# A two-block transformer forward pass: the first keys and values formed chunk by chunk while the modulation weights arrive

## The chip, the cores and the metric

The kernel runs on one core of a Trainium2 chip. TensorE multiplies matrices, ScalarE (ACT in the profile) applies functions, VectorE (DVE) does elementwise work, GpSimd (POOL) copies, and SyncE (SP) issues most of the DMAs. The metric is the device time of one execution in microseconds (us).

## What is computed

Two model blocks follow each other on 256 tokens of width 1024. The first has two layers, each with attention, a long convolution, gates and a feed-forward part, and works on `x` and on 256 context tokens. The second ends in a mixture of 32 experts. The change concerns the very start of layer 0, cut from the reference here:

```python
mod = (silu_c @ w_mod[layer] + b_mod[layer])[:, None, :]
mod_c = silu_cc @ w_mod[layer] + b_mod[layer]
shift1, scale1, gate1, shift2, scale2, gate2 = jnp.split(mod, N_MOD, axis=-1)
h_ctx = modulate(rms_norm(ctx, norm_mix[layer]), c_shift1, c_scale1)   # h*(1+scale)+shift
qc, kc, vc, hyc, gc = jnp.split(h_ctx @ w_in[layer], PROJ_SPLITS, axis=-1)
h = modulate(rms_norm(x, norm_mix[layer]), shift1, scale1)
q, k, v, hy, g = jnp.split(h @ w_in[layer], PROJ_SPLITS, axis=-1)
```

## The kernel before

Activations lie with features on the partitions: `X` is 8 chunks of 128 features by 512 tokens (`x` and the context side by side), 2 MB. Every engine has its own program, written by hand in order, and engines meet by semaphores; nothing is reordered.

**The modulation.** `shift1` and `scale1` need 16 columns of 128 of `w_mod`. They come as 16 units of 512 KB (`first`), into `area`, `HH` and `KX`. Four units make a group: `pe_mod_group` multiplies the two conditions by them (8 matmuls, L629), ScalarE copies the result (`ac_mod_group`, L653), and `pe_mod_turn` turns it into columns (4 matmuls, L645). Groups 0 and 1 hold the eight shift columns, groups 2 and 3 the eight scale columns, so no chunk of `X` can be modulated before group 3 is turned. Then `ve_mod_groups` adds the bias (L662) and forms the scale (L669).

**The norm.** ScalarE squares the eight chunks (L575), VectorE adds seven of them (L551), TensorE sums over features (L535, L542), ScalarE takes the root (L587), VectorE the reciprocal (L598), TensorE spreads it (L558), and VectorE multiplies each chunk of `X` into `H` (L882).

**A chunk's last steps.** ScalarE scales and shifts it in two halves (L863). GpSimd (L875), or for chunks 2 and 5 ScalarE (L868), rounds it to the high part `HH`. VectorE forms the low part `HL` (L890). A projection is three matmuls for each product: high by high, high by low, low by high.

**The weights** of the projections come as 512 KB units through a ring of six places. ScalarE makes the high part of each unit in one of three places (`his`, L453), VectorE the low part (L461). Units 0 and 1 are the keys' weights, 2 and 3 the values', 4 on the queries'. A place comes free when the product that read it is done.

**The projections.** `pe_idle` first runs 12 matmuls on ones, whose result nobody reads (L570). `pe_pair` forms both key heads over the eight chunks (6 matmuls of 512 columns for each chunk, L497), `pe_head_sums` sums the squares of key head 0 (L521), `pe_values_projected` forms the values (12 matmuls of 256 columns for each chunk, L948), and a second sum follows. Then come the eight query heads, 24 matmuls each (L482).

**The loads.** SyncE issues in this order: four units of `w_mod`, `X` whole, eight units of `w_mod`, units 0 and 1 of `w_in`, four of `w_mod`, unit 2, the constants of the transforms (1347 KB), units 3 to 5, then two tables into `area` for the filter.

## Time and profile before

| | |
|---|---|
| Median of 3 runs | 2072.62 us (2068.78 to 2075.53) |
| The profiled execution's own time | 2071.54 us |
| Its span | 2069.7 us |
| TensorE busy | 1880.4 us, 91% |
| VectorE busy | 1155.6 us, 56% |
| ScalarE busy | 903.6 us, 44% |
| DMA moved | 428.01 MB, 207 GB/s over the span |
| First key matmul starts | 40.06 us |

The span runs from the first to the last instruction, and 1.8 us of the execution's time lie around it. A busy TensorE is not one at full rate: its clock has two levels, shown as granted clock 1.00 (2.4 GHz) and 0.50 (1.2 GHz). Times below count from the start of the span. An fp32 matmul shows as two instructions in the rows, so "x8" there is four matmuls.

### The profile page before, as it was taken

The numbers are of one execution on the slowest core, as the hardware profiler recorded it, in microseconds if no ns is written. First come the engines' busy times: TensorE is split into PE (matmuls) and PEld (weight loads), VectorE is DVE, ScalarE is ACT, GpSimd is POOL, SyncE is SP. The second block draws the span as 40 slices with busy tenths as digits, with TensorE's granted clock in tenths as the row PEclk, the third lists the DMA queues.
The fourth block names the chain that finished last, engine by engine and source line by source line (L and its number), as shares of the span: only waits on it lengthen the run. The fifth ranks groups of instructions, "written<-read, shape, count | busy, mean of one in ns | idle before, by whom it ended". The sixth has DMA issues, their size and how long they took to land.

```text
span 2069.7 us, 33760 instructions
## 1 busy us (share of the span) xinstructions
PE 1880.4 (91%) x14150; PEld 1547.8 (75%) x14150; DVE 1155.6 (56%) x1898; ACT 903.6 (44%) x1532; POOL 17.0 (1%) x31
## 2 busy tenths in 40 slices
PE   7999989999999999999999999999999777767666
PEld 4877668888778888798699999997898544445444
DVE  3555767775887788567666667689764111110012
ACT  4333446665766677455455556644844000000001
POOL 0000000000000000000000000000000000000000
PEclk8999999999999999999999999999999998998888
DMA  8222024553555555224056555543248999999996
GB/s 315 92 72 82 1 72 157 181 184 106 175 175 181 195 192 174 101 93 153 1 184 204 180 187 194 175 159 107 92 143 340 419 420 421 419 419 420 420 421 249
DMA packets 91121, 428.01 MB, mean 207 GB/s; under 512 B 11089, under 2 KB 12754, under 8 KB 66002
## 3 DMA queue, kind: packets, MB, share of 16 engines
q1 hardware_dynamic: 78866, 382.51, 49.5%
q10 hardware_dynamic: 12096, 43.26, 6.2%
q8 instruction: 114, 1.87, 0.4%
q14 instruction: 45, 0.37, 0.1%
HBM read 424.68 MB, written 1.05 MB: 206 GB/s over the span
## 4 chain that ended last, share of the span: by engine, by line
PE 65%; DMA 19%; DVE 8%; ACT 5%; issue 2%; SPq 1%; ACTq 0%; DVEq 0%
PE bank L482 42%; DMA area<-in_w 8%; PE bank L1629 8%; DMA his<-in_w 4%; DMA ring<-in_w 4%; DMA PPT<-in_w 3%; PE bank L497 2%; PE bank L2518 2%; PE bank L2474 1%; DVE st L1280 1%; PE bank L1208 1%; ACT PPT L1225 1%; PE bank L948 1%; DVE ring_r L461 1%; PE bank L2125 1%
## 5 line engine op out<-in xcount | busy, mean ns | idle before, releaser
L461 DVE TENSOR_TENSOR ring_r<-ring,his_r 128x1024 fp32r<-128x1024 f32 x314 | 383.3, 1223 | 220.9 <-ACT his_r L453 219.6
L482 PE MATMUL bank<-HH_r,his_r 128*128 128x256 f32 (+1 forms) x1504 | 497.1, 331 | 2.5 <-DVE ring_r L461 2.5
L482 PE MATMUL bank<-HH_r,ring_r 128*128 128x256 f32 (+1 forms) x1504 | 489.3, 325 | 0.0
L482 PE MATMUL bank<-H_r,his_r 128*128 128x256 f32 (+1 forms) x1440 | 470.3, 327 | 0.0
L453 ACT ACTIVATE his_r<-ring 128x1024 fp32r<-128x1024 f32 x314 | 330.8, 1056 | 292.8 <-PE bank L482 262.6
L482 PEld LDWEIGHTS bank<-HH_r,his_r 128*128 128x128 f32 x1504 | 284.4, 189 | 35.0 <-issue 9.6
L482 PEld LDWEIGHTS bank<-HH_r,ring_r 128*128 128x128 f32 x1504 | 284.2, 189 | 24.8
L482 PEld LDWEIGHTS bank<-H_r,his_r 128*128 128x128 f32 x1440 | 271.4, 188 | 25.2 <-issue 1.0
L2490 DVE TENSOR_TENSOR tmp<-tmp,bank 128x128 f32<-128x128 f32 x64 | 18.4, 288 | 385.3 <-ACT tmp L2483 255.3
L482 PE MATMUL bank<-area_r,his_r 128*128 128x256 f32 (+1 forms) x480 | 148.3, 321 | 0.0
L2474 PE MATMUL bank<-area,KF 128*32 128x128 f32 x1888 | 88.1, 308 | 38.2 <-DMA area<-in_w 33.2
L1629 PE MATMUL bank<-VT_r,his_r 128*128 128x512 f32 (+1 forms) x352 | 117.2, 333 | 0.3 <-DVE YF_r L1360 0.3
L1629 PE MATMUL bank<-YF_r,his_r 128*128 128x512 f32 (+1 forms) x352 | 117.0, 333 | 0.0
L1629 PE MATMUL bank<-VT_r,ring_r 128*128 128x512 f32 (+1 forms) x352 | 117.0, 333 | 0.0
L2474 PEld LDWEIGHTS bank<-area,KF 128*32 128x32 f32 x1888 | 71.4, 124 | 51.9 <-DMA area<-in_w 41.9
L482 PEld LDWEIGHTS bank<-area_r,his_r 128*128 128x128 f32 x480 | 90.4, 191 | 6.9
L2529 ACT ACTIVATE H<-bank 128x512 f32<-128x512 f32 x16 | 9.6, 598 | 193.5 <-PE bank L2518 193.5
L731 ACT ACTIVATE rst<-rst 128x1024 f32<-128x1024 f32 x80 | 83.6, 1046 | 1.7 <-DVE rst L723 1.6
L2518 PE MATMUL bank<-area,tmp 128*32 128x512 f32 x256 | 59.3, 682 | 19.1 <-DMA area<-in_w 18.7
L1629 PEld LDWEIGHTS bank<-VT_r,his_r 128*128 128x128 f32 x352 | 66.1, 188 | 7.3 <-DVE YF_r L1360 0.5
L1629 PEld LDWEIGHTS bank<-YF_r,his_r 128*128 128x128 f32 x352 | 66.1, 188 | 6.9
L1629 PEld LDWEIGHTS bank<-VT_r,ring_r 128*128 128x128 f32 x352 | 66.1, 188 | 6.9
(415 smaller groups left out, 3309.2 us busy)
## 6 DMA issues: line engine op xcount, KB each, us to landing
area<-in_w SPq DMA_DIRECT2D x91, 1024.0 KB, 27.5
ring<-in_w_in SPq DMA_DIRECT2D x102, 512.0 KB, 3.5
ring<-in_w_gate_up SPq DMA_DIRECT2D x88, 512.0 KB, 3.5
ring<-in_w SPq DMA_DIRECT2D x36, 1024.0 KB, 27.3
HH<-in_w SPq DMA_DIRECT2D x26, 1024.0 KB, 26.7
ring<-in_w_down SPq DMA_DIRECT2D x44, 512.0 KB, 3.5
KX<-in_w_mod_rows ACTq DMA_DIRECT2D x28, 512.0 KB, 3.4
VX<-in_w_mod_rows ACTq DMA_DIRECT2D x28, 512.0 KB, 3.5
```

The lines of the kernel that those rows point to most:

```text
L453: ac.eng.activation(hi_slot(n), stream.slot(u), ACT.Copy).then_inc(*ac_hi.up(n))
L461: ve.eng.tensor_tensor(lo_slot(u), stream.slot(u), hi_slot(n).bitcast(F32), ALU.subtract).then_inc(*ve_lo.up(n))
L482: ins = pe.eng.matmul(out, a, b, start=k == 0 and m == 0, stop=end)
L497: ins = pe.eng.matmul(out, a, b, start=k + m == 0, stop=k == 7 and m == 2)
L731: ac.eng.activation(prod, prod, ACT.Copy, accum_out=MODS[l][:, j, s:s + 1]).then_inc(*ac_mod.up("sum", n, s))
L948: ins = pe.eng.matmul(vb[tb // 2][:, o:o + 256], x[:, k, sl], w, start=k == 0 and n == 0 and o == 0, stop=k == 7 and n == 2 and o > 0)
L1208: ins = pe.eng.matmul(out[:, 0:256], vs(kc), c.pts[g % 2][:, kc * 256:(kc + 1) * 256], start=kc == 0, stop=kc == c.nk - 1)
L1225: ac.eng.activation(p[:, m * w:(m + 1) * w], src[:, m * w:(m + 1) * w], ACT.Exp, bias=st[:, so + m:so + m + 1], scale=c.rq(h, i + m) if c. ...
L1280: ve.eng.reduce_max(st[:, so:so + c.n], src.rearrange("p (a b) -> p a b", a=c.n), AX.X, negate=True).then_inc(*ve_soft.up("max", c.site, h ...
L1629: ins = pe.eng.matmul(banks.ap("ff", l, 4 * half + n)[:, 0:t], w, x, start=k == 0 and i == 0, stop=k == 21 and i == 2)
L2474: ins = pe.eng.matmul(out[32 * n:32 * n + 32, 0:P], HG[g % 2][:, k, 32 * j:32 * j + 32], w, start=k == 0, stop=k == 7, tile_position=(0, 3 ...
L2518: ins = pe.eng.matmul(out[32 * j:32 * j + 32, :], AT[j][:, 32 * k:32 * k + 32], w, start=k == 0, stop=k == 3, tile_position=(0, 32 * j))
```

## The change

Six things are changed, all before or in the first projections of layer 0; layer 1 and the rest keep their order.

- **Groups.** The columns of `w_mod` are permuted (`FIRST_MOD`), so that group g holds shift and scale of chunks 2g and 2g+1. `ve_mod_first` forms these after each turn: three small instructions a group, twelve in place of three.
- **Loads.** `X` comes first, in two halves. Units 0 and 1 of `w_in` follow the first group, unit 2 the second, unit 3 the third. The transforms' constants come behind unit 5, and the filter's tables wait for group 3, since `w_mod` lies where they go.
- **Places.** `w_mod` no longer uses `HH`, which is written early now; it uses `area`, `VX` and `KX`. The high parts of units 3, 4 and 5 get places of their own in `VT` and `KF`, which stand idle until the convolution filter.
- **Order.** `pe_start`, `ac_start` and `ve_start` replace the written-out beginning. Keys and values go side by side, chunk by chunk, between the modulation's groups.
- **Dummy work.** `pe_idle` is not called.
- **Sums of the keys.** Both follow query head 0 (i = 2) in place of standing around the values, and the root, the reciprocal and the spreading move one head later.

```diff
+HIGH_ELSEWHERE = range(NHI, 2 * NHI)
+FIRST_MOD = [j for g in range(4) for j in (2 * g, 2 * g + 1, 8 + 2 * g, 9 + 2 * g)]
...
-        first = Stream([("w_mod", 0, u) for u in range(16)], [area[:, i * UF:(i + 1) * UF] for i in range(11)] +
-                       [hh_flat[:, i * UF:(i + 1) * UF] for i in range(4)] + [KX_flat[:, :]], [sem(f"s_m{i}") for i in range(16)], UB)
+        first = Stream([("w_mod", 0, u) for u in range(16)], [area[:, i * UF:(i + 1) * UF] for i in range(14)] + [VX_flat[:, :], KX_flat[:, :]], [sem(f"s_m{i}") for i in range(16)], UB)
...
         def hi_slot(n):
-            at = n % NHI * UW + stream.leads[cut_units[n]]
+            lead = stream.leads[cut_units[n]]
+            if n in HIGH_ELSEWHERE:
+                tile, at = ((VTR, 0), (KFR, 0), (KFR, UF))[n - NHI]
+                return tile.rearrange("p a t -> p (a t)")[:, at + lead:at + lead + UF]
+            at = n % NHI * UW + lead
             return his[:, at:at + UF]
+
+        def hi_before(n):
+            return n - NHI if n >= 3 * NHI else n - 2 * NHI
...
-            if g > 0:
-                pe_mod_turn(pe, g - 1)
-            if g == 3:
-                pe_mod_turn(pe, g)
-                banks.give("mods")
...
-        def ve_mod_groups(ve):
-            ve.wait_ge(*pe_mod.at("turn", 3))
-            ve_mod_bias(ve, 0, 0, 16, banks.ap("mods")[:, 0:32].rearrange("p (j s) -> p j s", s=2))
-            ve_mod_scale(ve, 0, 0)
+        def ve_mod_first(ve, g):
+            chunks = slice(2 * g, 2 * g + 2)
+            src = banks.ap("mods")[:, 0:32].rearrange("p (w k s) -> p w k s", w=2, s=2)
+            dst = MODS[0][:, 0:16, :].rearrange("p (w k) s -> p w k s", w=2)
+            bias = vv(("b_mod", 0), 0, 16).rearrange("p (w k) -> p w k", w=2)
+            ve.wait_ge(*pe_mod.at("turn", g))
+            for w in range(2):
+                ve.eng.tensor_tensor(dst[:, w, chunks, :], src[:, w, chunks, :], bias[:, w, chunks].unsqueeze(2).to_broadcast([P, 2, 2]),
+                                     ALU.add).then_inc(*ve_mod.up(*(("first", g) if w else ("shift", g))))
+            ve.wait_ge(*ve_mod.last())
+            ve.eng.scalar_tensor_tensor(A12S[0][:, 0, chunks, :], dst[:, 1, chunks, :], 1.0,
+                                        vv(("norm_mix", 0), 2 * g, 2).unsqueeze(2).to_broadcast([P, 2, 2]), ALU.add,
+                                        ALU.mult).then_inc(*ve_mod.up("first_scale", g))
...
+        def pe_start(pe):
+            pe_mod_group(pe, 0)
+            pe_open(pe, "mix0")
+            pe_added("mix0")
+            pe.wait_ge(*gp_start.at("ones"))
+            pe_sum_seven(pe, "mix0", 512)
+            pe_sum_last(pe, "mix0", 512)
+            pe_mod_turn(pe, 0)
+            pe_spread(pe, "mix0", 512)
+            pe_mod_group(pe, 1)
+            keys = [(("head", 0, i), head_bank(pe, 0, i), 8 * pos[8 + i]) for i in range(2)]
+
+            def pe_keys_chunk(k):
+                pe_pair_chunk(pe, keys, "w_in", 0, k, lambda k: (HH[:, k, 0:512], HL[:, k, 0:512]),
+                              lambda k: pe.wait_ge(*ve_norm.at("low", "mix0", k)))
+
+            pe_keys_chunk(0)
+            pe_keys_chunk(1)
+            pe_mod_turn(pe, 1)
+            pe_values_open(pe, 0)
+            pe_values_chunk(pe, 0, 0)
+            pe_values_chunk(pe, 0, 1)
+            pe_mod_group(pe, 2)
+            for k in range(2, 8):
+                pe_keys_chunk(k)
+                pe_values_chunk(pe, 0, k)
+                if k == 2:
+                    pe_mod_turn(pe, 2)
+                    pe_mod_group(pe, 3)
+                if k == 3:
+                    pe_mod_turn(pe, 3)
+
+        def ac_start(ac):
             for k in range(8):
...
+                ac.wait_ge(*landed[f"x{k // 4}"])
+                ac_square(ac, "mix0", k, X[:, k, :], 512)
+            ac_sqrt_table(ac, 5, 8)
+            ac_mod_group(ac, 0)
+            ac_split(ac, where["w_in", 0, 0])
+            ac_sqrt(ac, "mix0", 8, 512, 1024)
+            ac_split(ac, where["w_in", 0, 1])
+            ac_first_chunk(ac, 0)
+            ac_first_chunk(ac, 1)
+            ac_mod_group(ac, 1)
+            ac_split(ac, where["w_in", 0, 2])
+            ac_first_chunk(ac, 2)
+            ac_first_chunk(ac, 3)
+            ac_split(ac, where["w_in", 0, 3])
+            ac_mod_group(ac, 2)
+            ac_first_chunk(ac, 4)
+            ac_mod_group(ac, 3)
+            for k in (5, 6, 7):
+                ac_first_chunk(ac, k)
+            ac_split(ac, where["w_in", 0, 5])
+
+        def ac_first_chunk(ac, k):
+            ac.wait_ge(*ve_mod.at("first_scale", k // 2))
+            ac_norm_chunk(ac, "mix0", 0, 512, k)
+
+        def ve_start(ve):
+            for k in range(1, 7):
+                ve_add_square(ve, "mix0", k, 512)
+            ve_reciprocal(ve, "mix0", 512)
+            ve_split(ve, where["w_in", 0, 0])
+            ve_mod_first(ve, 0)
+            ve_split(ve, where["w_in", 0, 1])
+            r = spread_out(ve, "mix0", 512)
+            for k in range(4):
+                ve_scaled(ve, "mix0", k, 512, r)
+            ve_norm_low(ve, "mix0", 512, 0)
+            ve_norm_low(ve, "mix0", 512, 1)
+            ve_scaled(ve, "mix0", 4, 512, r)
+            ve_scaled(ve, "mix0", 5, 512, r)
+            ve_split(ve, where["w_in", 0, 2])
+            ve_mod_first(ve, 1)
+            ve_scaled(ve, "mix0", 6, 512, r)
+            ve_scaled(ve, "mix0", 7, 512, r)
+            ve_norm_low(ve, "mix0", 512, 2)
+            ve_norm_low(ve, "mix0", 512, 3)
+            ve_split(ve, where["w_in", 0, 3])
+            ve_mod_first(ve, 2)
+            ve_norm_low(ve, "mix0", 512, 4)
+            ve_mod_first(ve, 3)
+            for k in (5, 6, 7):
+                ve_norm_low(ve, "mix0", 512, k)
+            ve_split(ve, where["w_in", 0, 5])
...
         def pe_heads(pe, l):
-            pe_pair(pe, [(("head", l, i), head_bank(pe, l, i), 8 * pos[8 + i]) for i in range(2)], "w_in", l,
-                    lambda k: (HH[:, k, 0:512], HL[:, k, 0:512]), lambda k: pe.wait_ge(*ve_norm.at("low", f"mix{l}", k)))
-            pe_head_sums(pe, l, 0)
-            pe_values_projected(pe, l)
-            pe_head_sums(pe, l, 1)
+            if l:
+                pe_pair(pe, [(("head", l, i), head_bank(pe, l, i), 8 * pos[8 + i]) for i in range(2)], "w_in", l,
+                        lambda k: (HH[:, k, 0:512], HL[:, k, 0:512]), lambda k: pe.wait_ge(*ve_norm.at("low", f"mix{l}", k)))
+                pe_head_sums(pe, l, 0)
+                pe_values_projected(pe, l)
+                pe_head_sums(pe, l, 1)
             for i in range(2, 10):
                 pe_head(pe, l, i)
-                if i < 4:
-                    pe_spread(pe, head_site(l, i - 2), 512)
+                if l == 0 and i == 2:
+                    pe_head_sums(pe, l, 0)
+                    pe_head_sums(pe, l, 1)
+                if 3 - l <= i < 5 - l:
+                    pe_spread(pe, head_site(l, i - 3 + l), 512)
...
-            ac_sqrt(ac, head_site(l, 0), 1, 512, P)
+            if l:
+                ac_sqrt(ac, head_site(l, 0), 1, 512, P)
...
             for i in range(2):
                 ve_split(ve, two_on(unit("w_in", l, 8 * pos[heads(l)[i][0]])))
-            ve_reciprocal(ve, head_site(l, 0), 512)
+            if l:
+                ve_reciprocal(ve, head_site(l, 0), 512)
             ve_rope_step(ve, l, 0)
             for b in (10, 11):
                 ve_split(ve, two_on(unit("w_in", l, 8 * pos[b])))
-            ve_reciprocal(ve, head_site(l, 1), 512)
+            if l:
+                ve_reciprocal(ve, head_site(l, 1), 512)
             ve_rope_step(ve, l, 1)
+            if l == 0:
+                ve_split(ve, two_on(unit("w_in", l, 8 * pos[0])))
+                for i in range(2):
+                    ve_reciprocal(ve, head_site(l, i), 512)
             for i in range(2, 10):
                 ve_split(ve, two_on(unit("w_in", l, 8 * pos[heads(l)[i][0]])))
-                if i < 4:
-                    ve_key(ve, l, i - 2)
+                if 3 - l <= i < 5 - l:
+                    ve_key(ve, l, i - 3 + l)
...
-            pe_mod_group(pe, 0)
-            pe_mod_group(pe, 1)
-            pe_open(pe, "mix0")
-            pe_added("mix0")
-            pe.wait_ge(*gp_start.at("ones"))
-            pe_sum_seven(pe, "mix0", 512)
-            pe_sum_last(pe, "mix0", 512)
-            pe_spread(pe, "mix0", 512)
-            pe_mod_group(pe, 2)
-            pe_mod_group(pe, 3)
-            pe_idle(pe, "mix0", 12)
+            pe_start(pe)
...
-            ac_mod_group(ac, 0)
-            ac.wait_ge(*landed["x"])
-            for k in range(8):
-                ac_square(ac, "mix0", k, X[:, k, :], 512)
-            ac_mod_group(ac, 1)
-            ac_sqrt_table(ac, 5, 8)
-            ac_sqrt(ac, "mix0", 8, 512, 1024)
-            ac_mod_group(ac, 2)
-            ac_split(ac, where["w_in", 0, 1])
-            ac_mod_group(ac, 3)
-            ac_norm_mod(ac, "mix0", 0, 512)
+            ac_start(ac)
...
-            for k in range(1, 7):
-                ve_add_square(ve, "mix0", k, 512)
-            r = ve_rstd(ve, "mix0", 512)
-            for k in range(8):
-                ve_scaled(ve, "mix0", k, 512, r)
-            ve_split(ve, where["w_in", 0, 1])
-            ve_mod_groups(ve)
-            ve_norm_mod(ve, "mix0", 0, 512)
+            ve_start(ve)
...
+            for half in range(2):
+                sp.eng.dma_start(X[:, 4 * half:4 * half + 4, :], T["x"][:, 4 * half:4 * half + 4, :]).then_inc(*landed[f"x{half}"])
             for i, (name, l, u) in enumerate(first.units):
                 if i == 4:
-                    sp.eng.dma_start(X[:, :, :], T["x"]).then_inc(*landed["x"])
-                if i == 12:
                     weights(0)
                     weights(1)
+                if i in (8, 12):
+                    weights(i // 4)
                 sp.eng.dma_start(first.slot(i), T[name][l, u]).then_inc(first.arrived(i)[0], 16)
-            weights(2)
-            sp.eng.dma_start(con[:, NCON0:NCON], T["con"][:, NCON0:NCON]).then_inc(*landed["dft"])
-            for i in range(3, len(stream.units)):
+            for i in range(4, len(stream.units)):
                 if i == NS:
+                    sp.eng.dma_start(con[:, NCON0:NCON], T["con"][:, NCON0:NCON]).then_inc(*landed["dft"])
+                    sp.wait_ge(*pe_mod.at("group", 3))
                     sp.eng.dma_start(FIN, T["fil"]).then_inc(*landed["fil0"])
                     sp.eng.dma_start(FW, T["fw"][0]).then_inc(*landed["fw0"])
...
-    arrays["w_mod"] = fours(I["w_mod"][0:1, :, 0:2048])
+    arrays["w_mod"] = fours(I["w_mod"][0:1].reshape(1, 1024, 48, P)[:, :, FIRST_MOD].reshape(1, 1024, 2048))
```

`pe_pair_chunk`, `pe_values_chunk`, `ac_norm_chunk` and `ve_norm_low` are the bodies of the old loops, for one chunk.

TensorE at the start, before, from the first turn to the first key matmul (`bank0` collects the turned columns, `HH_r` and `H_r` are high and low part of the chunks, `his_r` and `ring_r` of the weights):

```order
L645 MATMUL bank0<-con,PPT 128x2 x4
L535 MATMUL bank3<-ones,tmp2 128x1 x4
L542 MATMUL bank3<-ones,tmp1 128x1 x4
L558 MATMUL bank3<-con,st 128x128 x4
L629 MATMUL bank4<-area,sc2 32x512 x6
L629 MATMUL bank4<-HH,sc2 32x512 x2
L645 MATMUL bank0<-con,PPT 128x2 x4
L629 MATMUL bank5<-HH,sc2 32x512 x6
L629 MATMUL bank5<-KX,sc2 32x512 x2
L645 MATMUL bank0<-con,PPT 128x2 x8
L570 MATMUL bank6<-ones 128x128 x12
L497 MATMUL bank7<-HH_r_50,his_r_62 128x512
```

The same engine after, up to the fourth group:

```order
L651 MATMUL bank0<-con,PPT 128x2 x4
L569 MATMUL bank2<-con,st 128x128 x4
L640 MATMUL bank3<-area,sc2 32x512 x8
L508 MATMUL bank4<-HH_r_50,his_r_62 128x512
...
L651 MATMUL bank0<-con,PPT 128x2 x4
L977 MATMUL bank6<-his_r_62,HH_r_50 128x256
...
L640 MATMUL bank1<-area,sc2 32x512 x8
L508 MATMUL bank4<-HH_r_50,his_r_62 128x512
...
L651 MATMUL bank0<-con,PPT 128x2 x4
L640 MATMUL bank2<-area,sc2 32x512 x4
```

The first keys stand behind group 1 (`bank3`), the first values behind turn 1, two further keys and values between groups 2 and 3; before, all stood behind turn 3 and the dummy matmuls.

VectorE at the same place, before, from the reciprocal of the norm:

```order
L598 RECIPROCAL st<-st 128x4
L882 TENSOR_TENSOR H<-X,bank3 128x512 x8
L461 TENSOR_TENSOR ring_r_61<-ring,his_r_62 128x1024 x2
L662 TENSOR_TENSOR MOD0<-bank0,vec 128x32
L669 SCALAR_TENSOR_TENSOR A120<-MOD0,vec 128x8 x2
L890 TENSOR_TENSOR H_r_49<-H,HH_r_50 128x512 x8
L1023 TENSOR_SCALAR qg<-vec 128x1
```

And after, from the same reciprocal:

```order
L609 RECIPROCAL st<-st 128x4
L469 TENSOR_TENSOR ring_r_61<-ring,his_r_62 128x1024
L670 TENSOR_TENSOR MOD0<-bank0,vec 128x4 x2
L673 SCALAR_TENSOR_TENSOR A120<-MOD0,vec 128x4
L469 TENSOR_TENSOR ring_r_61<-ring,his_r_62 128x1024
L902 TENSOR_TENSOR H<-X,bank2 128x512 x4
L912 TENSOR_TENSOR H_r_49<-H,HH_r_50 128x512 x2
L902 TENSOR_TENSOR H<-X,bank2 128x512 x2
L469 TENSOR_TENSOR ring_r_61<-ring,his_r_62 128x1024
L670 TENSOR_TENSOR MOD0<-bank0,vec 128x4 x2
L673 SCALAR_TENSOR_TENSOR A120<-MOD0,vec 128x4
```

The first low parts (`H_r_49`) now stand behind two weight splits, the first group's three small instructions and four scaled chunks; before they stood behind all eight.

## Rows read from the trace of the kernel before

**Rows 1.** The page: DMA busy tenths in 40 slices, then the last chain by engine.
```profile
DMA  8222024553555555224056555543248999999996
...
PE 65%; DMA 19%; DVE 8%; ACT 5%; issue 2%; SPq 1%; ACTq 0%; DVEq 0%
```

**Rows 2.** TensorE weight loads, window 5 to 37 us: start, us, what, [idle, releaser].
```profile
9.00 0.14 PEld L629 LDWEIGHTS bank<-area,sc 128*32 128x32 f32 x4 [1.05 <-DMA area<-in_w_mod]
15.19 0.19 PEld L629 LDWEIGHTS bank<-area,sc 128*32 128x32 f32 x4 [6.05 <-DMA area<-in_w_mod]
...
19.03 0.14 PEld L629 LDWEIGHTS bank<-area,sc 128*32 128x32 f32 x4 [1.10 <-DMA area<-in_w_mod]
...
32.96 0.14 PEld L629 LDWEIGHTS bank<-KX,sc 128*32 128x32 f32 x4 [1.12 <-DMA KX<-in_w_mod]
```

**Rows 3.** ScalarE, window 13 to 37 us, same columns.
```profile
13.88 1.15 ACT L575 ACTIVATE tmp<-X 128x512 f32<-128x512 f32 x2 [3.19 <-DMA X<-in_x]
...
19.57 0.63 ACT L575 ACTIVATE tmp<-X 128x512 f32<-128x512 f32 x1 [0.16 <-DVE tmp L551]
...
20.75 1.28 ACT L580 ACT_TABLE_LOAD   x1
...
29.93 1.99 ACT L453 ACTIVATE his_r<-ring 128x1024 fp32r<-128x1024 f32 x2
```

**Rows 4.** TensorE, window 19 to 41 us, same columns.
```profile
20.93 1.03 PE L535 MATMUL bank<-ones,tmp 128*128 128x1 f32 x8
21.82 1.33 PE L542 MATMUL bank<-ones,tmp 128*128 128x1 f32 x8
23.72 2.08 PE L558 MATMUL bank<-con,st 128*128 128x128 f32 x8 [0.57 <-DVE st L598]
25.73 2.78 PE L629 MATMUL bank<-area,sc 128*32 128x512 f32 x10
...
29.30 1.05 PE L645 MATMUL bank<-con,PPT 128*128 128x2 f32 x8
30.28 1.06 PE L629 MATMUL bank<-HH,sc 128*32 128x512 f32 x8
```

**Rows 5.** VectorE, window 25 to 41 us, same columns.
```profile
25.84 4.87 DVE L882 TENSOR_TENSOR H<-X,bank 128x512 f32<-128x512 f32 x8 [2.17 <-PE bank L558]
31.08 2.36 DVE L461 TENSOR_TENSOR ring_r<-ring,his_r 128x1024 fp32r<-128x1024 f32 x2 [0.38 <-ACT his_r L453]
35.93 0.19 DVE L662 TENSOR_TENSOR MOD<-bank,vec 128x32 f32<-128x32 f32 x1 [2.49 <-PE bank L645]
36.16 0.24 DVE L669 SCALAR_TENSOR_TENSOR A<-MOD,vec 128x8 f32<-128x8 f32 x2
38.23 0.69 DVE L890 TENSOR_TENSOR H_r<-H,HH_r 128x512 fp32r<-128x512 f32 x1 [1.83 <-POOL HH_r L875]
```

**Rows 6.** Last chain, window 32 to 80 us: start, us, what.
```profile
35.89 4.41 PE bank L570 x24
40.30 10.24 PE bank L497 x45
...
52.91 11.41 PE bank L948 x96
64.33 0.78 PE bank L521 x8
65.11 5.58 PE bank L482 x24
```

**Rows 7.** Three windows: length, busy by engine, granted clock, DMA share, GB/s.
```profile
22.70:29.10 6.40, 5.83 (x27) 2.75 (x26) 3.44 (x7) 0.26 (x1) 0.00 (x0) 0.50 1.03 410
36.50:39.70 3.20, 3.20 (x18) 3.20 (x18) 0.96 (x2) 3.17 (x7) 1.44 (x2) 0.54 1.04 416
40.00:50.00 10.00, 10.00 (x47) 8.30 (x46) 5.47 (x9) 6.66 (x13) 2.91 (x4) 1.00 0.24 73
```

**Rows 8.** SyncE queue, window 1555 to 1600 us: start, us, what it issues.
```profile
1562.44 0.43 SPq L2911 DMA_DIRECT2D con<-in_w  x1
```

112 lines of the change are left out of this document (64 added, 48 removed).

## The prediction

> **What bounds the kernel now.** The page comes first. The chain that ended last is TensorE for 65% and DMA for 19%, and the row of DMA shares shows where the DMA part lies: the last nine slices are full, the middle is at a fifth to a half, and the first slice is full too [rows 1]. So there are three stretches. A filled queue bounds the start, TensorE the long middle, the experts' weights the end. The change is in the first.
>
> The start is read next, by what TensorE's weight loads wait for. The units of `w_mod` let them go at 9.0 us for the fourth, 15.2 for the fifth, 19.0 for the eighth and 33.0 for the sixteenth [rows 2]. ScalarE finds `X` landed at 13.9 us and ends the eight squares at 20.2 [rows 3]. TensorE has little to do meanwhile: sums, spreading, groups, turns [rows 4]. VectorE has scaled all of `X` by 30.7 us and then stands until the turn lets it form the scales at 35.9 [rows 5]. The last chain puts it together: dummy matmuls of 4.4 us, keys from 40.3, values, the sums of the keys, query head 0 from 65.11 to 70.69 [rows 6]. At 70.69 both key heads, their sums, the values and query head 0 are done. That mark is the one to compare: after the change the same work is done when query head 0 and the two sums behind it are.
>
> **The arrivals after the change.** The same bytes pass the same queue, so a unit's time goes by its place. 2 MB stand ahead of the moment 9.0 (four units), and 4 MB ahead of 13.9. With `X` in front it has landed whole at about 9.0 in place of 13.9, and group 0 is complete at 13.9 in place of 9.0. Behind that, the first four places take 1.28 us each (15.2 to 19.0), the ten up to 33.0 take 1.39 [rows 2]. Unit 0 and 1 of `w_in` take places 1 and 2; group 1 is complete at place 6, 19.0 + 2 x 1.39 = 21.8; unit 2 at 23.2; group 2 at place 11, 28.8; unit 3 at 30.2; group 3 at place 16, 33.0 + 2 x 1.39 = 35.7, which is 2.8 us later than now. The norm starts earlier: the squares took 6.3 us from `X` to the last [rows 3], with the halves of `X` landing near 6.4 and 9.0 they end by 13, and the table load of 1.3 ends by 14.5. Both are covered by group 0, and if they slipped by over 0.5 us they would push what follows one for one.
>
> **TensorE up to the first keys.** Group 0 ends 1.1 us behind its last unit, at 15.0. The two sums take 2.2 us (20.93 to 23.15), so 17.2. Root and reciprocal take 0.6 (23.15 to 23.72) beside turn 0, which takes 1.0, so 18.2. Spreading takes 2.1: 20.3. Group 1 took 3.6 us at the low clock (25.73 to 29.30): 23.9 [rows 4], its data being there by 21.8. VectorE reaches the first low part by another path: reciprocal at 17.8, a weight split 1.2, the group's three small instructions 0.5, a second split 1.2, four scaled chunks 4 x 0.61 = 2.4, one low part 0.7, together 23.8 [rows 5]. Through ScalarE and GpSimd the same chunk takes 1.8 us from its scales to the low part's start [rows 5]: scaled at 21.3, ready for the low part at 23.1. The three paths meet at 23.9, so TensorE starts the keys there, 16.4 us earlier than now.
>
> **From the keys on.** Eight chunks of both keys took 10.24 us for 45 instructions seen, 0.228 each, so a chunk of six is 1.37; the values took 11.41 for 96, so a chunk of twelve is 1.43 [rows 6]. Together 2.8 us a chunk. A group at the high clock: four units of which two took 1.06 with their tail [rows 4], the four about 1.9. Then:
> Keys 0 and 1, 2.7: 26.6. Turn 1, 1.0: 27.6. Values 0 and 1, 2.9: 30.5. They need unit 2 split; VectorE gets to it behind the second low part and two scaled chunks, and ends at 27.5, in time. Group 2, 1.9: 32.4 (data at 28.8). Chunk 2 of both, 2.8: 35.2. Its low part follows turn 1 by 0.5 for the scales, 1.3 for two scaled chunks and about 1.8 and 0.7 for the chunk's own steps, 31 at the most. Turn 2: 36.2. Group 3, whose data is there at 35.7: 38.1. Chunk 3: 40.9. Turn 3: 41.9. Chunks 4 to 7, 4 x 2.8: 53.1. Chunk 5's low part stands behind turn 3 on VectorE, ready at 43.1, needed at 44.7. Chunk 7's comes 2.1 (two chunks on ScalarE, 1.0 each) + 0.8 + 0.7 behind the scales at 42.4, so near 46.5, needed at 50. Query head 0, 5.6, and two sums of 0.8 to 0.9: 60.3.
>
> Nothing that is moved comes late by this. The wait of SyncE for group 3 ends at 38.1, and the constants (1347 KB, at 512 KB in 1.39 us) occupy the queue until 42. Units 6 to 9 go out when key head 0 is done at 52, as they now go out at 50.6, and unit 6 is needed behind head 1, near 67. The four splits on ScalarE (1.0 each, [rows 3]) fit beside: it has 13 of the 29 us from 24 to 53 free.
>
> **The sum.** 70.7 - 60.3 = 10.4 us. The steps above leave nothing between one kind of work and the next. Two groups of the last chain that follow on each other, the values' end at 64.32 and the sum at 64.33, leave nothing either [rows 6], but a joint that crosses engines does (the turn's small instruction on VectorE starts at 35.93 and the next at 36.16, 0.04 behind its end, [rows 5]), and several more ones wait for a semaphore and a matmul's tail: I count 0.1 each. For eight such joints I take off 0.8, an estimate. **9.6 us** remain. From 80 us on, TensorE goes on as before. The tail moves with it: the first expert's load is issued at 1562.44 [rows 8], behind the last units of the ring, and these wait for TensorE's products. 2071.5 - 9.6 = 2061.9 for a profiled execution; the median of the runs is 1.1 above it, so 2063.0.
>
> **The clock, and a rule against the change.** TensorE ran at the low level from 22.7 to 29.1 us, behind the sums with one column, and mostly at it from 36.5 to 39.7, behind two turns with two columns; from 40 to 50 it was at the high one [rows 7]. The dummy matmuls stood before the keys, and the keys ran at the high level. They are gone now, and turns stand in the middle of the work. The price of a low stretch is half its length: 1.6 us for one of 3.2, 3.2 for one of 6.4. I take the high level from 23.9, since group 1 and the spreading before it are as dense as what preceded the rise at 29.1.
> The Trainium skill ("TensorE: Matmul & The Clock Gate", "What's actually happening" and "Why this matters for your kernels") calls the half rate the default that activity releases, and advises to keep matmuls back to back. By that, waits and turns between the chunks, with the dummies gone, would leave parts of the keys and values at half rate. The fall at 22.7 agrees with it; how much of it strikes the new order no row shows.
>
> **The rivals.**
> *A low stretch strikes the chunks.* Two of 3.2, or one of 6.4 us, within 24 to 53: 3.2 us lost, gain 6.4, **2066.2**. For it: both falls in the rows follow turns or sums. Against: here one turn at a time stands between 2.7 us of dense work. Chance 0.20.
> *The low parts come late.* VectorE, ScalarE and GpSimd hand each chunk on three times, and a slip before 27.6 us passes in full to the end. Three us of waits in all: **2066.0**. For it: VectorE's path to the first keys (23.8) has no slack to TensorE's. Chance 0.13.
> *Slower: the whole stretch at the low clock.* From 23.9 to 53.1 lie 29.2 us, of which turns take 3.0 (one took 1.05 at the high level, and it is weight loads, so I count it constant). If the other 26 us doubled, the kernel would be 26 - 9.6 = 16 us slower, **2089**. It decides at 19 us of low clock. Against: the longest low stretch in the rows is 6.4 us, and it ended under groups alone. Chance 0.05.
> *It does not reach the end.* If the experts' stream did not start earlier, full queues at the end would give all back: **2072**. Against it stands that SyncE has waits of its own for TensorE just before 1562. Chance 0.06.
>
> **How the numbers follow.** Forecast 0.56, 2063.0, with a range of its own of 2060.5 to 2066. The range that is to hold 8 in 10 reaches from 2059 (the joints cost nothing, and the runs fall on the low side of their spread of 6.8) to 2069 (a low stretch and late parts together, or runs on the high side). A change of 0.3%, 6.2 us, is about what a measurement of this kernel can tell from none. Faster by more than that, below 2066.4: 0.54 of the forecast, 0.11 of the clock's 0.20, 0.10 of the late parts, 0.75. Within: 0.20. Slower: 0.05.
>
> **What will show it.** The first key matmul at 24 us, not 40.3. The sixteenth unit of `w_mod` at 35.7. Keys, values and head 0 with two sums done at 60 to 61. Granted clock 1.00 in most of 24 to 53; any 0.50 there is the first rival. TensorE waiting on VectorE's low parts (L912) for over 1 us is the second. The first expert's load at about 1553 in place of 1562.4. The forecast is wrong if the first two hold and the mark at 60 does not, or if the mark holds and 1553 does not.

## The result, and the profile after

| | kernel before | changed kernel |
|---|---|---|
| median of the first comparison (6 runs each) | 2069.97 us | 2058.51 us (2056.45 to 2065.73) |
| ratio, 95% interval | | 0.9946 [0.9926, 0.9967] |
| profiled execution, its span | 2071.5, 2069.7 us | 2065.73, 2063.9 us |
| first key matmul | 40.06 us (40.30 in the last chain) | 24.64 us |
| mark: keys, values, query head 0 and both sums done | 70.69 us | 60.91 us |
| first expert's load issued | 1562.44 us | 1556.44 us |

The change makes the kernel faster by 0.54%, some 11 us. The profiled execution of after is the slowest of its six, so the trace shows less at the end than the median does; that is taken up below. First the last chain of after, window 0 to 72 us (start, us, what); it answers to [rows 6], and in part to [rows 2 to 5].

```profile
10.59 5.67 PE bank L640 x16
16.26 1.13 PE bank L546 x8
17.39 0.91 PE bank L553 x8
...
18.71 1.21 DVE ring_r L469
...
20.18 1.23 DVE ring_r L469
21.40 0.61 DVE H L902
...
22.09 1.10 ACT H L883 x2
...
23.25 0.62 POOL HH_r L895
...
23.90 0.70 DVE H_r L912
...
24.64 3.04 PE bank L508 x12
27.68 0.79 PE bank L651 x8
28.47 2.83 PE bank L977 x24
31.30 1.85 PE bank L640 x16
33.15 1.59 PE bank L508 x6
...
53.78 5.45 PE bank L490 x24
59.23 1.68 PE bank L532 x16
60.91 5.59 PE bank L490 x24
```

Three stretches are to be seen. Up to 16.3 TensorE follows the queue: four units, 5.7 us, of which the last 1.9 are the fourth unit's own work after it landed at 14.34. From 18.7 to 24.6 the chain leaves TensorE and runs over VectorE's two weight splits (L469), one scaled chunk (L902) and the chunk's high and low parts. From 24.64 it is TensorE alone, without a gap, up to the mark: two chunks of keys 3.04, a turn 0.79, two chunks of values 2.83, a group 1.85. Before, the keys only began at 40.06.

TensorE's weight loads of the same stretch ([rows 2] of before) show which unit it waits for:

```profile
14.34 0.19 PEld L640 LDWEIGHTS bank<-area,sc 128*32 128x32 f32 x4 [1.09 <-DMA area<-in_w_mod]
...
20.20 0.20 PEld L640 LDWEIGHTS bank<-area,sc 128*32 128x32 f32 x8 [0.22 <-issue]
21.06 0.18 PEld L640 LDWEIGHTS bank<-area,sc 128*32 128x32 f32 x2 [0.66 <-DMA area<-in_w_mod]
```

The last unit of group 0 is there at 14.34; within group 1 there is one more wait, and behind it none on a unit of `w_mod`.

The windows of after, which answer to [rows 7] (length, busy by engine, granted clock, DMA share, GB/s):

```profile
0.00:10.40 10.40, 0.00 (x0) 0.00 (x0) 2.09 (x6) 3.97 (x8) 0.48 (x7) 1.00 0.82 314
10.50:20.00 9.50, 9.41 (x48) 4.57 (x48) 3.87 (x8) 6.47 (x10) 0.00 (x0) 1.00 1.03 410
20.20:23.40 3.20, 3.20 (x17) 0.68 (x16) 3.20 (x6) 1.30 (x3) 0.15 (x1) 0.51 1.03 410
23.40:53.80 30.40, 29.47 (x205) 24.11 (x202) 15.18 (x30) 15.76 (x27) 3.97 (x6) 1.00 0.69 262
```

The first two windows can't be taken as they stand, since the trace has no record of the clock before 16.5 us and the windows print 1.00 for what has none. The matmuls themselves tell the level. These are the same instructions of L640 in three stretches, from 10.4 to 16.5 (group 0), 20 to 23 (group 1, 0.50 granted) and 30 to 34 us (group 2, 1.00 granted), with the shortest, median and longest duration in ns:

```profile
L640 PE MATMUL bank<-area,sc x16: 1030/1061/1062, 10.6 to 15.2; 128*32 128x512 f32 x16
L640 PE MATMUL bank<-area,sc x16: 831/1061/1062, 20.2 to 22.9; 128*32 128x512 f32 x16
L640 PE MATMUL bank<-area,sc x16: 592/592/617, 31.2 to 32.6; 128*32 128x512 f32 x16
```

So TensorE ran at the low level twice: over all of group 0, and again from 19.9 to 23.4, behind sums, turn and the start of the spreading. The second stretch lies over group 1, where TensorE had time: it then waited for the low part. From 23.4 to 53.8 the granted clock is 1.00 throughout.

### The profile page after: what moved, and what is told of

It is laid out like the page before. It is cut to its first block, busy times and chain, and to the rows that moved or that the text cites. A ratio compares the mean times of both kernels' runs of the same rounds, so it can differ in the third digit from the quotient of the medians.

```text
span 2063.9 us, 33725 instructions
## 1 busy us (share of the span) xinstructions
PE 1875.5 (91%) x14126; PEld 1546.4 (75%) x14126; DVE 1156.3 (56%) x1907; ACT 903.5 (44%) x1532; POOL 16.8 (1%) x31
## 3 DMA queue, kind: packets, MB, share of 16 engines
HBM read 424.68 MB, written 1.05 MB: 206 GB/s over the span
## 4 chain that ended last, share of the span: by engine, by line
PE 62%; DMA 20%; DVE 10%; ACT 5%; issue 2%; ACTq 0%; POOL 0%; DVEq 0%; SPq 0%; POOLq 0%
PE bank L490 39%; PE bank L1760 8%; DMA area<-in_w 8%; DMA his<-in_w 4%; DMA ring<-in_w 4%; DMA PPT<-in_w 4%; PE bank L2649 2%; PE bank L508 2%; DVE ring_r L469 1%; PE bank L2605 1%; DVE st L1411 1%; PE bank L1339 1%; ACT PPT L1356 1%; PE bank L977 1%; DVE area L2100 1%
## 5 line engine op out<-in xcount | busy, mean ns | idle before, releaser
L469 DVE TENSOR_TENSOR ring_r<-ring,his_r 128x1024 fp32r<-128x1024 f32 x311 | 379.8, 1223 | 216.4 <-ACT his_r L461 215.2
L490 PE MATMUL bank<-HH_r,his_r 128*128 128x256 f32 (+1 forms) x1488 | 492.0, 331 | 2.4 <-DVE ring_r L469 2.4
L490 PE MATMUL bank<-H_r,his_r 128*128 128x256 f32 (+1 forms) x1424 | 465.2, 327 | 0.0
L2605 PE MATMUL bank<-area,KF 128*32 128x128 f32 x1888 | 91.4, 321 | 42.4 <-DMA area<-in_w 36.3
L1487 ACT ACTIVATE VT_r<-area 128x512 fp32r<-128x512 f32 (+1 forms) x96 | 50.0, 523 | 49.9 <-PE bank L1760 44.5
```

Of the source, the lines that this page charges most:

```text
L469: ve.eng.tensor_tensor(lo_slot(u), stream.slot(u), hi_slot(n).bitcast(F32), ALU.subtract).then_inc(*ve_lo.up(n))
L490: ins = pe.eng.matmul(out, a, b, start=k == 0 and m == 0, stop=end)
L1487: ac.eng.activation(hi, src, ACT.Copy).then_inc(*ac_cut.up(*key))
L2605: ins = pe.eng.matmul(out[32 * n:32 * n + 32, 0:P], HG[g % 2][:, k, 32 * j:32 * j + 32], w, start=k == 0, stop=k == 7, tile_position=(0, 3 ...
```

## Experiments

"Mark" is the time at which both key heads, their sums, the values and query head 0 are done, "first key" the first matmul of L508 (L497 before). A ratio stands with its 95% interval and goes against runs of the kernel before in the same group. Diffs are cut to their core.

**The two kernels again.** No edit.

> The changed kernel once more, unaltered. In its profile the mark (query head 0 and both key sums done) came at 60.9 us against 70.7 before, 9.8 us, but its whole execution was 5.8 us shorter. From 1166 to 1310 us it lost 4.5 us, where TensorE's matmuls of layer 1 started every 0.118 us in place of 0.113. Theory one: this pace has two values that come and go between executions of any kernel. Then the mark is at 60.9 +- 0.2 again, the pace may be either, and an execution near 2057 shows 0.113 there and one near 2064 shows 0.118. Theory two: the change itself makes layer 1 slower, by what it leaves behind. Then the pace is 0.118 again whatever the time is.

> The kernel before once more, unaltered. Theory one (a pace with two values in any kernel): the mark at 70.7, and either pace in layer 1, with some 2069.5 for 0.113 and 2074 to 2076 for 0.118. Theory two (the change causes the slow pace): 0.113 in every execution of this one.

The changed kernel took 2059.96 us, ratio 0.9949 [0.9936, 0.9963], first key 23.56, mark 59.82, no low stretch of the clock on record from 13.9 to 75 us. The kernel before took 2069.1, ratio 0.9995 [0.9982, 1.0007], first key 39.00, mark 69.67. Its mark is 1.0 earlier than in the first trace because the 12 dummy matmuls ran at the high level and took 2.92 us, where they took 4.55 at the low one. A third group of runs of the changed kernel:

> The changed kernel a third time, unaltered, to size the effect beside fresh runs of the kernel before. So far the ratios were 0.9946 and 0.9949, that is 10.5 to 11.2 us, and the marks 60.9 and 59.8. Theory (the gain is what the start gains, 9.8 us at the mark, and the rest is the clock elsewhere and the pace of layer 1, which vary between executions): ratio 0.993 to 0.997, mark 59.5 to 61.2. Rival (the gain grows behind the start): the shift against the kernel before's trace, point by point, grows again behind the mark by over 1 us and stays.

It took 2060.55, ratio 0.9945 [0.9931, 0.9959], mark 60.22. So the marks are 70.69 and 69.67 before (mean 70.18), and 60.91, 59.82, 60.22 and, in a fourth trace further down, 60.23 after (mean 60.30). **9.9 us are gained at the mark**; by single traces it would be 8.8 to 10.9.

The four marks of the changed kernel differ by 1.1 us, and nearly all of it is there when group 0 ends, at 16.26, 15.32, 15.73 and 15.75. From there to the mark it takes 44.5 to 44.7 in every trace. The fourth unit of group 0 landed within 0.2 us (14.15 to 14.34), but its work took 1.92 us in the first trace, where all of it ran at the low level, 1.05 in the second, at the high one, and 1.5 to 1.6 in the two others.

**The dummy matmuls, taken out of the kernel before and put back into the changed one.** They compute nothing that is read.

```
             pe_mod_group(pe, 3)
-            pe_idle(pe, "mix0", 12)
```

> The kernel before without the 12 dummy matmuls. Theory one (they only fill a wait): the first low part was formed at 38.9 and the first key matmul then starts at about 39.0 in place of 40.06, and the mark comes 1.1 us earlier if the clock is the same. Rival (the clock): without them the keys start at the low level, 0.43 us for a matmul of 512 columns in place of 0.228; over 3.4 us of low clock that costs 1.7, and the mark is at 71.3, 0.6 later than now.

It took 2070.55, ratio 0.9996 [0.9984, 1.0007]. The last chain and one window:

```profile
39.01 12.77 PE bank L497 x45
...
66.35 5.58 PE bank L482 x24
...
37.00:44.00 7.00, 4.99 (x12) 3.94 (x13) 3.62 (x6) 6.94 (x15) 2.89 (x4) 0.51 0.80 285
```

Without the dummies the keys wait for the low part and start at 39.01, 1.05 us earlier than the 40.06 of the first trace of before and no earlier than the 39.00 of the second, but from 37 to 44 us the granted clock is 0.51, and 45 matmuls take 12.77 in place of 10.24 us. The mark is 71.92, 1.2 to 2.3 later than with them. In this execution, of the old order, the first rival of the prediction was right. It is one trace, of the slowest of ten executions (2075.79 us), and the medians don't differ, so what the dummies save on average isn't shown.

```
             pe_mod_group(pe, 1)
 
+            pe_idle(pe, "mix0", 12)
             pe_keys_chunk(0)
```

> The changed kernel with the 12 dummy matmuls put back ahead of the first keys. TensorE waited 0.9 us there for the first low part, and the clock was at the high level from 23.4 us on. Theory (nothing is left for them to warm): they add their length less that wait, 2.2 to 3.5 us; the mark at 63.3 to 64.4. Rival (the clock would fall without them in other executions): the time is the same or shorter.

```profile
23.06 2.88 PE bank L581 x24
25.93 2.76 PE bank L508 x12
```

They take 2.88 us, in part in place of TensorE's wait for the low part (0.6 to 1.0 in the traces of the changed kernel). Mark 61.92, 1.0 to 2.1 later than there (2.1 against the second trace, which had no low stretch from 13.9 on either); the time was 2061.7, ratio 0.9958 [0.9946, 0.9971]. The two chunks of keys behind them took 2.76 in place of 3.04, so 0.3 comes back. The ratio's interval overlaps those of the changed kernel, so the cost is seen in the marks alone. By the traces the same dummies are worth what they take in the old order and a cost in the new one. That the full group ahead of the keys makes the difference, where the old order has turns and a wait, is an argument and wasn't tried by itself.

**`X` behind the four first units, as before.**

```
-            for half in range(2):
-                sp.eng.dma_start(X[:, 4 * half:4 * half + 4, :], ...)
             for i, (name, l, u) in enumerate(first.units):
                 if i == 4:
+                    for half in range(2):
+                        sp.eng.dma_start(X[:, 4 * half:4 * half + 4, :], ...)
```

> The changed kernel with X loaded behind the first four units of w_mod, as before, everything else as changed. Theory (arrivals and the norm's chain set the first keys): X lands at 13.9 in place of 8.9, squares end at 20.2, sums 22.4, and the first keys start 5 us behind those of the changed kernel (24.6), at 29 to 30; what follows is TensorE's own work, so the mark is at 64.5 to 66. Rival (the first keys' time does not matter because the fourth group's arrival at 35.7 sets the end): the mark stays within 1 us of 60.9.

```profile
18.32 1.84 PE bank L546 x8
20.16 1.71 PE bank L553 x8
21.87 1.71 PE bank L651 x8
23.57 1.93 PE bank L569 x8
...
28.86 3.03 PE bank L508 x12
```

The squares now end at 18.2, and the sums, the turn and the spreading behind them run at the low clock (0.50 from 12.9 to 26.5 us), 7.2 us together, where they took 3.8 to 4.0 in the first two traces of the changed kernel. First key 28.86, mark 65.11, 4.2 to 5.3 later. My expectation had the size, but not the cause: the sums start only 2.1 to 3.0 us later, since group 0 had covered the squares in the changed kernel, and some 3.3 come from the clock, behind a TensorE that stood idle for 7.9 us. (The two add up to 1.1 more than the first key's delay, since in the changed kernel VectorE's weight splits, here hidden, still stood ahead of it.) The time was 2065.67 us, ratio 0.998 [0.9964, 0.9995].

**All groups and turns first, then the chunks of keys and values side by side.** `X` stays in front.

```
-            pe_keys_chunk(0)
-            pe_keys_chunk(1)
             pe_mod_turn(pe, 1)
-            pe_values_open(pe, 0)
-            pe_values_chunk(pe, 0, 0)
-            pe_values_chunk(pe, 0, 1)
             pe_mod_group(pe, 2)
-            for k in range(2, 8):
+            pe_mod_turn(pe, 2)
+            pe_mod_group(pe, 3)
+            pe_mod_turn(pe, 3)
+            pe_values_open(pe, 0)
+            for k in range(8):
```

> The changed kernel with all four groups and turns ahead of the first keys on TensorE; loads, places and the side-by-side order of keys and values stay. Theory (the gain is the keys and values of chunks 0 to 3 done while w_mod arrives): TensorE waits for the last unit at 35.5, then 1.0, the last turn 1.0, and 22.3 us of keys and values, head 0 and the sums 7.1: the mark at 67 to 68.5, 6 to 7.5 us behind the changed kernel. Rival (order on TensorE matters little, the gain is the dummies and the early norm): the mark within 2 us of 60.9.

```profile
33.67 4.49 PE bank L640 x16
...
38.83 1.05 PE bank L651 x8
39.88 1.49 PE bank L508 x6
```

First key 39.88, mark 69.31, 8.4 to 9.5 later than after, and a little later than I expected; 2071.91 us, ratio 1.0009 [0.9994, 1.0024]. About 1 us of it is the clock: it was at 0.50 from 32.0 to 38.8, over the last group, whose last unit took 1.92 in place of 1.05. Nearly the whole gain hangs on work being done during the arrival: with `X` in front, but everything else behind the last group, the kernel is no faster than before.

**Keys as modulation arrives, all values behind them.**

```
             pe_mod_turn(pe, 1)
-            pe_values_open(pe, 0)
-            pe_values_chunk(pe, 0, 0)
-            pe_values_chunk(pe, 0, 1)
             pe_mod_group(pe, 2)
             ...
+            pe_values_open(pe, 0)
+            for k in range(8):
+                pe_values_chunk(pe, 0, k)
```

> The changed kernel with the values' matmuls all behind the keys', the keys still between the groups. Theory (side by side fills the waits for the groups): keys 0 and 1 end at 27.7, turn 1 at 28.5, group 2 has its last unit at 28.8, so the 2.8 us of values 0 and 1 are missing to fill; TensorE then has keys 2 to 4 (4.1 us) from 31.5 and waits for group 3 until 35.7; the mark 1 to 3 us behind the changed kernel. Rival (TensorE has enough with the keys alone): the mark within 0.5 us of 60.9.

```profile
36.13 1.05 PE bank L640 x4
...
42.61 3.01 PE bank L508 x12
```

Mark 64.06, 3.2 to 4.2 later, more than expected; 2062.56 us, ratio 0.9962 [0.9947, 0.9976]. The keys alone don't fill TensorE: it waits for the last unit of group 3 (landed by 36.1) and then, from 39.57 to 42.61, for the scales, high and low part behind the last turn. In the changed kernel the values stand in just these places.

**The two sums, at their old place in the changed kernel, and behind query head 0 in the kernel before.**

```
+            else:
+                pe_head_sums(pe, l, 0)
+                pe_head_sums(pe, l, 1)
             for i in range(2, 10):
                 pe_head(pe, l, i)
-                if l == 0 and i == 2:
-                    pe_head_sums(pe, l, 0)
-                    pe_head_sums(pe, l, 1)
```

> The changed kernel with both sums of the keys' squares in front of query head 0, not behind it. ScalarE had the second square ready at 54.0 in its trace, where the values ended at 53.8, and a sum takes 0.8. Theory (the sums move at no cost here, and the place saves nothing once the values end behind the keys): the mark within 0.4 us of the changed kernel's. Rival (TensorE waits for the squares and for the banks): 1 to 1.5 us later.

```profile
55.23 11.05 PE bank L490 x48
66.27 0.89 PE bank L569 x8
```

Sums and two heads end at 66.27; in the changed kernel (the last row shown above) at 60.91 + 5.59 = 66.50, in its second and third trace at 65.41 and 65.81. So the place of the sums costs nothing here, as expected. Yet the time was 2066.75, ratio 0.9976 [0.9963, 0.9989], 6.2 us above the changed kernel's in the same group. That is taken up in the last experiment.

In the kernel before the same move (sums of both key heads behind query head 0, with ScalarE's roots and VectorE's reciprocals moved after them):

```
-            pe_head_sums(pe, l, 0)
+            if l:
+                pe_head_sums(pe, l, 0)
             pe_values_projected(pe, l)
```

> The kernel before with one part of the change alone: both sums of the keys behind query head 0, with the root, reciprocal and spreading one head later. In its trace TensorE ended the keys at 50.55 and started the sum at 51.86, a wait of 1.3 us for ScalarE's square, which falls away. Theory: the mark 1.2 to 1.4 us earlier than 69.7 to 70.7 for the same start, counted from the first key matmul to the mark 29.3 in place of 30.6. Rival (the wait is only moved to the values' first matmuls): no difference.

```profile
39.28 11.18 PE bank L497 x48
50.46 11.31 PE bank L948 x96
```

The values follow the keys directly; in [rows 6] about 2.4 us lay between them, for the first key head's squares and its sum. From the first key to the mark it took 29.6 us, against 30.6 and 30.7 in the two traces of before: a gain of 1.0 to 1.1, a little less than I expected. The time was 2070.37, ratio 0.999 [0.9979, 1.0].

**Earlier splits, earlier spreading.** Two attempts to shorten the 8.4 us from group 0's end to the first key. In the first the weight splits stand ahead of the root and the reciprocal, in the second the spreading stands ahead of the turn too, and VectorE scales the first two chunks ahead of the group's three small instructions.

```
-            ve_reciprocal(ve, "mix0", 512)
             ve_split(ve, where["w_in", 0, 0])
+            ve_reciprocal(ve, "mix0", 512)
             ve_mod_first(ve, 0)
```

> The changed kernel with unit 0 of w_in split before the norm's root, on ScalarE ahead of group 0's copy and on VectorE ahead of the reciprocal. VectorE's path to the first low part (24.6 us) is 1.2 us shorter then, and TensorE's group 1 ends at 23.7. Theory (VectorE's path is the last to the first keys): first keys at 23.7 to 23.9, the mark 0.7 to 0.9 us earlier, 60.0 to 60.2. Rival (the pieces behind it are late anyway): the mark at 60.9.

```
-            pe_mod_turn(pe, 0)
             pe_spread(pe, "mix0", 512)
+            pe_mod_turn(pe, 0)
```

> The early split once more, and the norm is spread ahead of turn 0 on TensorE, with the first two chunks scaled ahead of the group's three small instructions on VectorE. With the early split alone, the first keys started 7.9 us behind group 0's end in place of 8.2 to 8.4, and spreading had become the last to come. Theory (the first low part is what the keys wait for): 7.4 to 7.7 us from group 0's end to the first key, and the mark 0.3 to 0.8 earlier than the changed kernel's, counted the same way; in the ratio that is too little to see. Rival (group 1's arrival at 22 holds the keys): 7.9 again.

The first took 7.9 us from group 0's end (15.96) to the first key (23.90), mark 60.15, 2061.56 us, ratio 0.9948 [0.9934, 0.9962]. That is 0.3 to 0.5 us less to the first key than in the four traces of the changed kernel (8.2 to 8.4), half of what I expected, and nothing that the time shows. The second was worse. Its chain and one window:

```profile
18.57 2.03 PE bank L569 x8
20.60 1.50 PE bank L651 x8
22.10 3.51 PE bank L640 x16
...
18.60:25.60 7.00, 7.00 (x33) 4.06 (x33) 4.52 (x9) 2.08 (x4) 1.44 (x2) 0.51 1.03 410
```

Spreading, turn and group 1 all ran at the low clock, where group 1's 3.51 us are now what the keys wait for (busy without a gap up to 25.61). Mark 61.80, 2063.82 us, ratio 0.9955 [0.9939, 0.9971].

**A later stage.** Two things were left: the 6.2 us of the sums at once, which the first 66 us don't show, and ratios of the changed kernel that give a little more than 9.9 us. The traces differ in layer 1's feed-forward. Windows there (same columns as above), first of the two traces of before, then of the changed kernel's first and second trace:

```profile
1160.00:1200.00 40.00, 40.00 (x356) 40.00 (x355) 25.26 (x37) 19.96 (x29) 0.00 (x0) 1.00 0.57 191
...
1160.00:1200.00 40.00, 40.00 (x342) 40.00 (x341) 24.54 (x34) 19.24 (x30) 0.00 (x0) 1.00 0.54 188
...
1240.00:1300.00 60.00, 60.00 (x532) 60.00 (x531) 45.29 (x74) 37.40 (x64) 0.00 (x0) 1.00 0.58 195
```

```profile
1130.00:1210.00 80.00, 79.77 (x682) 79.60 (x681) 49.52 (x69) 40.61 (x57) 1.02 (x2) 1.00 0.55 183
1240.00:1300.00 60.00, 60.00 (x512) 60.00 (x511) 43.42 (x69) 37.76 (x69) 0.00 (x0) 1.00 0.59 187
```

```profile
1130.00:1210.00 80.00, 80.00 (x704) 80.00 (x704) 50.06 (x67) 41.95 (x58) 0.25 (x1) 1.00 0.55 191
1240.00:1300.00 60.00, 59.68 (x527) 59.48 (x526) 45.20 (x74) 41.26 (x75) 0.00 (x0) 1.00 0.57 194
```

In the two traces of the changed kernel the granted clock is 1.00 and TensorE is busy, yet it starts 682 matmuls in 80 us in the one and 704 in the other. From 1240 to 1300 it is 512 in the one and 532 in the first trace of before, 0.117 against 0.113 us each. The kernel before has both paces too: from 1160 to 1200 us it starts 356 matmuls in its first trace and 342 in its second, 0.112 and 0.117 us each. So the longer pace is not made by the change. The last three runs ask whether this follows the kernel: the changed kernel a fourth time, the sums at once again, and the changed kernel with 20 in place of 10 dummy matmuls at the entry of that stage, which compute nothing that is read.

```
-            pe_idle(pe, site, 14 if l == 0 else 10)
+            pe_idle(pe, site, 14 if l == 0 else 20)
```

> The changed kernel, unchanged, a fourth time. Three ratios so far are 0.9946, 0.9949 and 0.9945. If the gain is what the mark shows (9.9 us of 2070, ratio 0.9952), this one lies within 0.994 to 0.996.

> The kernel with both sums straight behind the values, again, beside the changed kernel in the same call. Its first 66 us cost nothing in the trace, but its median was 6.2 us above that of the changed kernel. Theory A, a cost of this kernel that lies behind the mark (TensorE's pace or clock later on): the median is again 4 to 8 us above the changed kernel's. Theory B, scatter between groups of runs: it is within 2 us, ratio 0.994 to 0.996.

> The changed kernel with 20 in place of 10 dummy matmuls behind the norm ahead of layer 1's feed-forward; they compute nothing that is read. Ten more at 0.12 us each would cost 1.2 us at most, and nothing where TensorE waits there anyway. Theory A: the pace of 0.118 us a matmul in that stage (4 to 5 us a run) is set by how the work ahead of it lies against a low stretch of the clock, so that this edit changes the odds: the median moves by more than 2 us either way, and the trace shows 704 matmuls from 1130 to 1210 us where the change applies, 682 where not. Theory B: the pace falls by chance in any kernel: the median moves by 0 to 1.5 us.

| | median, us | ratio, interval | mark or its like | matmuls 1130 to 1210 | first expert's load |
|---|---|---|---|---|---|
| changed, fourth | 2060.91 (6) | 0.994 [0.9922, 0.9957] | 60.23 | 705 | 1551.31 |
| sums at once, again | 2064.6 (7) | 0.9955 [0.9938, 0.9971] | head 1 ends 65.61 | 685 | 1554.40 |
| more dummies | 2064.16 (6) | 0.9956 [0.9939, 0.9973] | 60.70 | 683 | 1556.43 |

The sums at once were 3.7 us above the changed kernel again, with a first part as fast (head 1 ends at 65.82 in the fourth trace of the changed kernel). Set beside that trace instruction by instruction on ScalarE, the sums at once are 1.0 us ahead at 1128 us and 4.4 behind at 1310: 5.4 us are lost in that stage, 1.5 come back by 1400 us, and the two executions differ by 3.0 in the end. So in these two the whole difference comes from that stage. The dummies came with 3.3 us. My expectation had priced them too low: ten take 2.40 us (1124.47 to 1126.87 in after, where a wait of 0.41 follows), so 2.0 of the 3.3 would be their own (the twenty took 4.63). Their trace lies 3.1 us behind the fourth trace of the changed kernel at 1128 us, and 2.5 of these come from 1050 to 1100 us, ahead of the dummies, where it starts 426 matmuls against 442: the longer pace again, at a place that the edit can't have reached by its own work. What stands is this. A cost of 3.7 to 6.2 us came twice with an edit that costs nothing at its own place, which speaks for the first theory, and one pair of traces puts it in layer 1. (The second time the intervals of the two ratios overlap.) Against it stands that the first trace of the sums at once had the short pace (706), with a median of 2066.75. The dummies decide nothing. What sets the pace, and whether it follows the kernel, is open.

## Why the prediction came out as it did

**What held.** The mechanism, step by step. Group 0 was forecast to end at 15.0 and ended at 15.3 to 16.3; the first key was forecast at 23.9 and came at 23.56 to 24.64; the mark, 60.3 by the steps and 61.1 with the joints, came at 59.82 to 60.91. A turn took 0.79 in place of 1.0 and the group behind it 1.85 (forecast 1.9). A turn's time is not constant, as the prediction had counted it: at the low level it took 1.77 (groups first). A chunk of keys took 1.36 to 1.6, one of values 1.4. The last unit was forecast at 35.7 and was there at 36.1 (keys first, where TensorE waits for it). The gain at the mark, 9.9 us between the means, was forecast as 9.6. From the first key to the mark the steps gave 36.4 us and it took 36.3 (60.91 - 24.64), so the 0.8 taken off for joints was not needed there. Part of the agreement at the first key is luck. Group 0's last unit was priced at 1.1 us, from [rows 2], where it ran at the high level; at the low one it takes 1.92. Spreading was priced at 2.1, from a low stretch, and took 1.0 to 1.2 in the first two traces. The two errors offset each other, and in all four traces the low part came last: in the chains of the four it is VectorE's, not TensorE's path that the keys follow. One thing was not foreseen and cost nothing: with 2 MB of `X` in front, `vec` landed later, ScalarE waited for it until 6.65 us, and the squares started only then. They ended at 13.2, still covered by group 0.

**The rivals.** No low stretch struck the chunks in any of the four traces of the changed kernel (1.00 from 23.4 us on to 53.8). The low parts came late by 0.6 to 1.0 us, in the one place where VectorE's path was said to have no slack (ahead of the first key), and the chunks behind didn't wait. The whole stretch at the low clock did not occur. The gain reached the end: the first expert's load was issued at 1562.44 [rows 8] and 1558.57 in the two traces of before and at 1556.44, 1550.84, 1552.85 and 1551.31 in the four of the changed kernel, 7.6 us earlier by the means.

**The step that failed is the level from which the sum was made.** The prediction put the median 1.1 us above the profiled execution, from three runs with a median of 2072.62. Six runs put it at 2069.97, and four later groups of 12 to 27 at 2070.04, 2070.78, 2071.06 and 2072.09. 2069.97 - 9.6 would have been 2060.4. The measured median, 2058.51, is 4.5 below the forecast: 2.65 of that are the level (2072.62 in place of 2069.97), 1.9 a gain of 11.5 in place of 9.6. The trace from which the sum starts was a draw as well: its mark, 70.69, has the dummies at the low level, and the second one is 69.67. The four medians of the changed kernel are 2058.51, 2059.96, 2060.55 and 2060.91; the first is the lowest and lies 0.5 below the lower end of the range. That end was made of joints that cost nothing and runs on the low side of their spread; an error of the level itself, 2 to 3 us with three runs, had no term in it.

**The gain beyond the mark.** The four ratios of the changed kernel, 0.994 to 0.9949, are 10.6 to 12.4 us of some 2070.8; the mark shows 9.9, a ratio of 0.9952. That lies within each of the four intervals, but above all four values. A different share of executions with the longer pace could make up the 1 to 2 us; that is open.

**The forecast for the tail failed in the profiled execution.** The expert's load was to be issued at 1553 and was at 1556.44. The windows above show why. Set beside the first trace of before instruction by instruction on VectorE, after is 10.3 us ahead at 1128 and 5.6 ahead at 1310: the longer pace of layer 1 took 4.7. In the three other traces the load is at 1550.84 to 1552.85.

**What each part brings**, read from what its removal costs the mark, in one trace each: work during the arrival 8.4 to 9.5, `X` in front 4.2 to 5.3, values beside keys 3.2 to 4.2, no dummies 1.0 to 2.1, the sums' place nothing. They rest on each other and don't add up to 9.9, and the first two have low stretches of the clock in them, about 1 us and some 3.3 us. The prediction had no such division; it had put the dummies' 4.4 us into the sum as a gain, and the kernel before without them shows that taking them out brings nothing by itself.

## What to carry to other kernels

Where a kernel starts with work that waits for a queue, cut the first products along the contraction and start each part when its scales are there; then lay a second product with the same operand beside the first, since one alone leaves the waits open. Judge a removed dummy matmul by what stands in its place: in the traces here it was pure cost behind dense work, and worth what it took behind small matmuls and a wait. For a forecast to 0.2%, three runs of the kernel before don't fix the level.

## What the runs showed of the hardware

**The clock at the start.** TensorE began at the low level. In after its first matmuls, from 10.6 to 15.2 us, have a median of 1061 ns, as at granted clock 0.50 from 20 to 23 us, against 592 at 1.00 from 30 to 34. The windows print 1.00 for this stretch, and for the 10.4 us in which TensorE did nothing, since the clock's records begin at 16.5 us in after, 13.9 in the second trace, 8.8 in before. Ahead of the first record only the durations tell. This agrees with the Trainium skill ("TensorE: Matmul & The Clock Gate", "What's actually happening"), which calls the half rate the default.

**The fall behind small matmuls.** From 16.6 to 19.9 us of after TensorE was at 1.00 and busy for 3.30 of 3.30 us with sums, turn and spreading; from 20.0 to 23.3 it was at 0.50. Before the fall at 22.4 to 22.7 of before it was busy for 3.40 of 3.40 us (19.0 to 22.4). The prediction read that fall as agreeing with the rule that it quotes there; the rows have a fall without a gap between the matmuls, so they don't bear that reading out. In the second trace of the changed kernel no fall followed the same sums, turn and spreading (1.00 from 20.0 to 23.3). What decides between the two wasn't found.

**Two paces at one clock.** With the granted clock at 1.00, 256-column matmuls that follow on each other started every 0.113 or every 0.117 us, in both kernels, for stretches of tens of us. Over layer 1's feed-forward the pace was worth 5.4 us between two executions (1.0 ahead at 1128 us, 4.4 behind at 1310), half of what this change brings. Its cause wasn't found.
